# A head of dilated attention with its projections in another order, the joint softmax ahead of the gate, and scores split by batch

## The reference

```python
A_GROUPS = ((128, 1), (512, 4), (2048, 16))          # window, dilation; 8 heads of 128 each
proj = h @ w_in                                       # q, k, v of each group, and the gate
for g, (window, dil) in enumerate(A_GROUPS):
    o, lse = dilated_window_attention(q, k, v, slopes[g], window, dil)   # ALiBi bias, softmax in the window
wts = softmax(stack(lses), axis=0)                    # a joint softmax over the three groups
o = sum(wts[..., None] * stack(outs))
y = o * silu(gate)
return y @ w_out
```

## Time and profile before

| | |
|---|---|
| median of 3 runs | 1840.05 us (1839.97 to 1840.76) |
| the profiled execution's own time | 1839.34 us |
| its span, first to last instruction | 1837.6 us |
| TensorE matmuls busy | 1748.7 us, 95% |
| VectorE busy | 1085.2 us, 59% |
| ScalarE busy | 726.6 us, 40% |
| GpSimd busy | 400.3 us, 22% |
| mean granted TensorE clock | 0.98 of full |

### The profile page before, as it was taken

One profiled execution on the slowest core, in us unless ns is written; L12 is line 12 of the kernel. 1 busy time (PEld: TensorE's weight loads), 2 busy tenths in 40 slices (PEclk: granted clock), 3 DMA queues, 4 the chain that ended last, 5 costly groups with the idle time before them and its releaser, 6 DMA issues. The chain is left out here.

```text
span 1837.6 us, 24762 instructions
## 1 busy us (share of the span) xinstructions
PE 1748.7 (95%) x8848; PEld 1478.6 (80%) x8848; DVE 1085.2 (59%) x1878; ACT 726.6 (40%) x1465; POOL 400.3 (22%) x320
## 2 busy tenths in 40 slices
PE   6999999999999999999999999689898999999995
PEld 5888888888888888888888888578686788888884
DVE  5344365355355445455445534653797898988986
ACT  5223323313312322322322322342215877777774
POOL 1001001001001001000100100111003877777764
PEclk9999999999999999999999999889899999999997
DMA  4111111111111011111111110020100000000002
GB/s 160 47 35 69 35 35 69 35 35 58 34 46 57 34 34 57 34 37 66 34 34 57 35 58 0 1 99 1 46 24 26 27 26 26 26 26 26 6 7 109
DMA packets 23241, 76.75 MB, mean 42 GB/s; under 512 B 3088, under 2 KB 3216, under 8 KB 22928
## 3 DMA queue, kind: packets, MB, share of 16 engines
q1 hardware_dynamic: 23184, 75.98, 12.1%
HBM read 71.77 MB, written 4.19 MB: 41 GB/s over the span
## 5 line engine op out<-in xcount | busy, mean ns | idle before, releaser
L701 PE MATMUL bankA<-hTh,wh 128*128 128x512 f32 x1280 | 505.4, 395 | 0.4 <-DVE hTl L477 0.4
L701 PE MATMUL bankA<-hTh,wl 128*128 128x512 f32 x1280 | 499.2, 390 | 0.0
L701 PE MATMUL bankA<-hTl,wh 128*128 128x512 f32 x1280 | 498.4, 389 | 0.0
L701 PEld LDWEIGHTS bankA<-hTh,wl 128*128 128x128 f32 x1280 | 240.2, 188 | 51.6
L701 PEld LDWEIGHTS bankA<-hTh,wh 128*128 128x128 f32 x1280 | 240.4, 188 | 48.6 <-issue 1.1
L701 PEld LDWEIGHTS bankA<-hTl,wh 128*128 128x128 f32 x1280 | 240.6, 188 | 47.9
L293 POOL TENSOR_TENSOR prob<-prob,wt_blk 128x1024 f32<-128x1024 f32 x16 | 32.3, 2020 | 1074.9 <-DVE wt_blk L601 1074.9
L527 DVE TENSOR_TENSOR qkl<-bankA,qkh 128x512 fp32r<-128x512 f32 x96 | 66.4, 692 | 287.7 <-ACT qkh L355 287.4
L355 ACT ACTIVATE qkh<-bankA 128x512 fp32r<-128x512 f32 x96 | 57.3, 596 | 367.2 <-PE bankA L701 367.2
L613 DVE TENSOR_TENSOR X<-bankA,X 128x512 f32<-128x512 f32 x128 | 83.9, 685 | 52.8 <-PE bankA L794 52.8
L503 DVE TENSOR_TENSOR wl<-raw,wh 128x1024 fp32r<-128x1024 f32 x78 | 102.8, 1318 | 15.7 <-ACT wh L325 13.3
(11 more groups left out here) (208 smaller groups left out, 3594.5 us busy)
## 6 DMA issues: line engine op xcount, KB each, us to landing
raw<-a_w_in SPq DMA_DIRECT2D x80, 512.0 KB, 3.3
bias<-alibi SPq DMA_DIRECT2D x8, 512.0 KB, 3.3
raw_out<-a_w_out SPq DMA_DIRECT2D x8, 512.0 KB, 4.1
graw<-b_w_gate SPq DMA_DIRECT2D x8, 512.0 KB, 3.6
raw_o<-b_w_out SPq DMA_DIRECT2D x16, 256.0 KB, 2.6
raw_q<-b_w_q SPq DMA_DIRECT2D x8, 384.0 KB, 4.0
X<-x_prompt SPq DMA_DIRECT2D x4, 512.0 KB, 5.5
X<-x_sample SPq DMA_DIRECT2D x4, 512.0 KB, 8.8
```

The costliest lines, as they stand in the source:

```text
L701: ins = pe.matmul(proj_ps[b][:, :], w[a][:, slot, k * P:(k + 1) * P], hT[c][:, k, b * S:(b + 1) * S], start=(i == 0), stop=(i == last))
```

## The change

The blocks q2 and k2 move ahead of v1 and the gate. The joint softmax moves from the end of the head to the end of v1, so it stands in the queues ahead of the gate. s1 is scored for batch 0 after k1 and for batch 1 after the first batch of q2; s2 after k2 and after the first batch of v1; s0 after each batch of v0. A dilated tile takes two matmuls: the high query by the high and low keys side by side (256 columns), and the low query by the high keys added into the first half; VectorE adds the bias to the first half, then the second half. The output rows stand beside q2, k2, the gate and v2; w_out is split after k1. After the last head a list (`LAST_TURNS`) orders transposes, weighting, rows and squares, and the mean and power of the first batch are made there, not in the next stage.

```diff
-PROJ = ["q0", "k0", "v0", "q1", "k1", "v1", "gate", "q2", "k2", "v2"]
+PROJ = ["q0", "k0", "v0", "q1", "k1", "q2", "k2", "v1", "gate", "v2"]
-ROW_SLOTS = [("gate", 0), ("gate", 1), ("q2", 0), ("q2", 1), ("k2", 0), ("k2", 1), ("v2", 0), ("v2", 1)]
+ROW_SLOTS = [("q2", 0), ("q2", 1), ("k2", 0), ("k2", 1), ("gate", 0), ("gate", 1), ("v2", 0), ("v2", 1)]
-SUMS = {"s0": 0, "s1": 4, "s2": 6}
+SUMS = {"s0": 0, "s1": 4, "s2": 8}
+LAST_TURNS = [("v2", 0), ("v2", 1), ("turn", 0, 0), ("turn", 0, 1), ("weigh", 0, 0), ("turn", 0, 2), ("weigh", 0, 1),
+              ("turn", 0, 3), ("weigh", 0, 2), ("turn", 1, 0), ("weigh", 0, 3), ("gated", 0), ("turn", 1, 1),
+              ("weigh", 1, 0), ("turn", 1, 2), ("row", 0), ("row", 1), ("weigh", 1, 1), ("turn", 1, 3),
+              ("row", 2), ("row", 3), ("weigh", 1, 2), ("row", 4), ("row", 5), ("weigh", 1, 3), ("gated", 1),
+              ("square", 0), ("row", 6), ("row", 7), ("square", 1), ("square", 2), ("square", 3), ("rate", 0)]
+for i_last in range(NT // 2, NT):
+    LAST_TURNS += [("row", 2 * i_last), ("row", 2 * i_last + 1), ("square", i_last)]
...
-        qk = [sb(f"qk{s}", [P, 2, NB, S], F32R) for s in "hl"]
+        qk_parts = sb("qk", [P, 2, 2, NB, S], F32R)
+        qk = [qk_parts[:, part] for part in (HI, LO)]
...
-        row_ps = sum_ps + out_ps
+        row_ps = proj_ps + sum_ps
...
@@ GpSimd, after the last head
+            pool.wait_ge(mean_ready, NB + 1)
+            pool.tensor_tensor(after["rstd"][:, 0:QT], after["ms"][:, 0:QT], minus_half[:, 0:QT],
+                               ALU.pow).then_inc(rstd_ready, 1)
...
@@ ScalarE, head
-                        if name == "v2" and b == 0:
+                        if name == "v1" and b == 0:
                             exps(h, 1, [1])
...
-                    if name == "v1" and not is_first(h):
+                    if name == "k1" and not is_first(h):
                         split_out(h)
...
-                factors(h)
+                    if name == "v1":
+                        factors(h)
...
@@ VectorE
+            def take_dilated(h, kind, b, step):
+                g = int(kind[1])
+                src = bias[:, (5 + g) * P:(6 + g) * P].unsqueeze(1).broadcast_to((P, 2, P))
+                def halves(pair):
+                    ps = sum_ps[sum_slot(kind, 2 * b + pair)][:].rearrange("p (t z k) -> p t z k", t=2, z=2)
+                    return prob[:, 1, b, 2 * pair:2 * pair + 2, (g - 1) * P:g * P], ps
+                for pair in range(2):
+                    at = sum_no(h, kind, 2 * b + pair)
+                    dve.wait_ge(sum_done, at + 1)
+                    dst, ps = halves(pair)
+                    ins = dve.tensor_tensor(dst, ps[:, :, 0], src, ALU.add)
+                chain(ins, h, step)
+                for pair in range(2):
+                    dst, ps = halves(pair)
+                    dve.tensor_tensor(dst, ps[:, :, 1], dst, ALU.add).then_inc(sum_taken, 1)
+                return at
...
-                        if (name, b) in (("k2", 1), ("v2", 0)):
-                            at = take_scores(h, "s2", 1 - b)
-                            maxima(h, 1, slice(1 - b, 2 - b), at, 6 - b)
-                    if name == "v0":
-                        for n in range(4):
-                            at = take_scores(h, "s0", n)
-                    if name == "v1":
-                        for b in range(NB):
-                            take_scores(h, "s1", b)
+                        if (name, b) in (("k2", 1), ("v1", 0)):
+                            at = take_dilated(h, "s2", 1 - b, 5 - 2 * b)
+                            maxima(h, 1, slice(1 - b, 2 - b), at, 6 - 2 * b)
+                        if name == "v0":
+                            for n in (2 * b, 2 * b + 1):
+                                at = take_scores(h, "s0", n)
+                        if (name, b) in (("k1", 1), ("q2", 0)):
+                            take_dilated(h, "s1", 1 - b, 2 - b)
...
-                joint_softmax(h)
+                    if name == "v1":
+                        joint_softmax(h)
...
+                elif step[0] == "rate":
+                    dve.wait_ge(row_squared, QT)
+                    dve.tensor_scalar(after["ms"][:, 0:QT], after["ss"][:, 0:QT], 1.0 / D, RMS_EPS, ALU.mult,
+                                      ALU.add).then_inc(mean_ready, 1)
...
@@ TensorE, score and output
-                    b = n
+                    b, pair = n // 2, n % 2
                     pe.wait_ge(proj_taken[b], proj_no(h, "k" + kind[1]) + 1)
-                    for t in range(QT):
-                        cols = slice(t * P, (t + 1) * P)
-                        for m, (x, z) in enumerate(SPLIT_PRODUCT):
-                            ins = pe.matmul(ps[:, cols], qk[x][:, 0, b, cols], qk[z][:, 1, b, cols],
-                                            start=(m == 0), stop=(m == 2))
+                    for i in range(2):
+                        cols = slice((2 * pair + i) * P, (2 * pair + i + 1) * P)
+                        at = 2 * P * i
+                        pe.matmul(ps[:, at:at + 2 * P], qk[HI][:, 0, b, cols], qk_parts[:, :, 1, b, cols],
+                                  start=True, stop=True)
+                        ins = pe.matmul(ps[:, at:at + P], qk[LO][:, 0, b, cols], qk[HI][:, 1, b, cols],
+                                        start=False, stop=True, skip_group_check=True)
...
+                    if is_past(h):
+                        if i % QT == 0:
+                            pe.wait_ge(y_split, h * 2 - 1 + i // QT)
+                    elif r == 0:
                         pe.wait_ge(y_split, h * 2)
...
@@ stage_b_in, VectorE
-            rate(0)
-            dve.wait_ge(rstd_ready, 1)
             scale(0, 0)
             scale(0, 1)
```

More of the change, by code:

```diff
@@ L91, in rows_beside, with last_row @@
     return [(r, r // NT, r % NT) for r in (2 * at, 2 * at + 1)]
-def last_rows():
-    return [(2 * i + half, half, i) for i in range(NT) for half in range(2)]
+def last_row(r):
+    return r, r % 2, r // 2
+LAST_TURNS = [("v2", 0), ("v2", 1), ("turn", 0, 0), ("turn", 0, 1), ("weigh", 0, 0), ("turn", 0, 2), ("weigh", 0, 1),
[5 more added lines that the diff above has]
+    LAST_TURNS += [("row", 2 * i_last), ("row", 2 * i_last + 1), ("square", i_last)]
 def row_no(h, r):
@@ L443, in _, with last_square @@
             split_out(A_HEADS)
-            for name in ("q0", "k0", "v0", "q1"):
-                for b in range(NB):
-                    between(A_HEADS, name, b)
-            for i in range(NT):
+            def last_square(i):
                 act.wait_ge(row_taken, row_no(A_HEADS, 2 * i + 1) + 1)
+                if i == 0:
+                    act.wait_ge(turned, turn_no(A_HEADS, "p", 7) + 1)
                 if i >= QT:
@@ L452, in _ @@
                 act.activation(scaled_x[:, i % QT, :], X[:, i, :], ACT.Square,
-                               accum_out=next_ss[:, i:i + 1]).then_inc(row_squared, 1)
+                               accum_out=after["ss"][:, i:i + 1]).then_inc(row_squared, 1)
+            for step in LAST_TURNS:
+                if step[0] == "gated":
+                    take_gated(A_HEADS, step[1])
+                elif step[0] == "square":
+                    last_square(step[1])
+                else:
+                    stand_between(A_HEADS, step)
         @block.vector
@@ L531, in take @@
                     gb = gate[:, b, :]
[L532 to L533 removed]
+                    chain(dve.tensor_scalar(gb, gb, 1.0, None, ALU.add), h, 13 + 2 * b)
+                    chain(dve.reciprocal(gb, gb), h, 14 + 2 * b)
                     dve.tensor_tensor(gb, ps, gb, ALU.mult).then_inc(proj_taken[b], 1)
@@ L668, in _ @@
             split_out(A_HEADS)
[L669 to L672, removed]
+            for step in LAST_TURNS:
+                if step[0] == "gated":
+                    take_gated(A_HEADS, step[1])
+                elif step[0] == "row":
+                    add_rows(A_HEADS, [last_row(step[1])], row_ps)
+                elif step[0] == "rate":
+                    dve.wait_ge(row_squared, QT)
+                    dve.tensor_scalar(after["ms"][:, 0:QT], after["ss"][:, 0:QT], 1.0 / D, RMS_EPS, ALU.mult,
+                                      ALU.add).then_inc(mean_ready, 1)
+                else:
+                    stand_between(A_HEADS, step)
         @block.tensor
@@ L817, in head @@
                                 output(h, rows_beside(name, b), out_ps)
[L818 to L825, removed]
+                        if (name, b) in (("k2", 1), ("v1", 0)):
+                            for pair in range(2):
+                                score(h, "s2", 2 * (1 - b) + pair)
+                        if (name, b) in (("k1", 1), ("q2", 0)):
+                            for pair in range(2):
+                                score(h, "s1", 2 * (1 - b) + pair)
+                        if name == "v0":
+                            for n in (2 * b, 2 * b + 1):
```

(14 more changed lines are left out.)

89 lines of the change are left out of this document (46 added, 43 removed).

## The result

The changed kernel takes 1847.6 us, the median of six runs (1846.7 to 1849.17), beside 1840.74 for the kernel before on the same chip: a ratio of 1.0042, 95% interval 1.0031 to 1.0052. Forecast were 1847 and "slower". The profiled execution has a span of 1845.4 us at a mean granted clock of 0.977.

A forecast was written before the change was run, and what follows sets the result against it. TensorE, busy 95% of the span, was taken to bound the kernel. Gains of 29.7 against losses of 37.3 gave 7.6 lost on 1839.34, so 1846.9; forecast 1847 us, range 1838 to 1868.

The forecast's parts named there:

- The stall: Softmax ahead of the gate on VectorE: TensorE idles 3.1 at row 10 in seven heads, 3.9 in the first; 25.6 lost.
- T+13.4: When TensorE finishes gate batch 1 and asks for row 10; T is when ScalarE begins to empty v1's second batch.
- The clock: TensorE at half speed for 3.1 after half of the row waits: 6 us lost, bounds nothing and 12.
- Scores apart: Dilated tiles: one 256-column and one 128-column product replace three of 128; 12.6 us gained, bounds nothing and 14.1.
- Block scores: A whole projection between the two batches' pairs removes TensorE's wait for VectorE's emptying: 4.1 us gained.
- v1 without cover: v1's transposes directly follow v1's projection, so the second batch's wait for ScalarE's copy: 0.44 x 8 = 3.5 us lost.
- Two more returns: Two more returns per head to a projection after transposes, 5.58 instead of 5.44: at most 2.2 us lost.
- End of the stage: Last projection to next stage's first scaling: earlier probability transposes and reordered row adds; 13 us gained, bounds 9.8 and 16.
- Rival 2: GpSimd's weighting holds VectorE up at the gate: 15 more idle and 6 more for the clock, 1868; chance 0.17.
- Rival 3: VectorE reaches row 8 before TensorE asks for row 10, so no wait arises: 24 gained, 1816; chance 0.12.

The follow-up runs named there:

- the filled wait: The changed kernel with 12 matmuls of 512 columns (16 in the first head), results unused, ahead of waiting row 10: 1834.52 us, ratio 0.9975.
- the kernel with the softmax under v2: The changed kernel with the joint softmax and ScalarE's `factors` moved behind the row adds of v2's first batch: 1811.44 us, ratio 0.9846.

## Why the prediction was right

The forecast, the stall with some of its clock, came true, and for the reason given: one place in VectorE's queue made the stall. That the time came within 1 us of 1847 is luck: the clock took twice what was forecast, and errors the other way cancelled it.

- *The stall*: forecast 7 x 3.1 + 3.9 = 25.6, measured 21.0 + 3.9 = 24.9. The row adds came when the working said; TensorE asked 0.27 later (568.91, where T+13.4 is 568.64).
- *The clock*: the term that was mis-sized, 6 forecast, 11 to 12 by the filled wait, the upper bound. Six stalls of eight lost the clock, not half of them, and the first two for longer (windows at 0.72 and 0.74, the other four at 0.87 or 0.88). The half came from a row that was read too short: of the idle that began at 1386.6 the prediction says that the clock held through it until 1390.4. But that idle lasted until 1393.92, and at 1390.4 the clock fell within it:

```profile
1393.92 0.80 PE L1670 MATMUL bankC<-cqTh,wqh 128*128 128x512 f32 x1 [7.39 <-DVE wql L1560]
```

So the row shows no idle that the clock outlasted. Nor would 3.8 at full clock have settled a stall of 3: four of the six falls came after TensorE had resumed.

- *Scores apart*: forecast 12.6; (1.31 - 0.87) x 32 batches is 14.1, the upper bound, and cutting the product again lost about 13 (1860.76 - 1847.6). The "1.8 to 1.9" that the prediction gives for eight products is its sum for sixteen, both batches.
- *Block scores*: the wait of 4.1 is gone, as forecast. *v1 without cover*: from the first transpose to the next projection 1.33 instead of 0.81 (555.04 to 556.37), 4.2 in eight heads, where 3.5 was forecast; the waits in it sum to 2.4. *Two more returns* do not show as the 2.2 allowed for: without the stall, a head of the kernel with the softmax under v2 lasts 141.33 (984.62 to 1125.95, ScalarE's copies of v2), before 143.50: 2.2 shorter, where these terms gave 1.4. Added up over a head from start to start of TensorE's matmuls, the dilated scores take 1.8 less and the block scores 0.8 less (3.8 before, 3.0 now; only their wait, 0.5, had been counted), the transposes 0.45 more, and projections and rows 0.1 less. That is all of the 2.2, and no return is in it.
- *A stall costs more than its wait*: a head in which the clock held lasts 144.7, 3.4 more than 141.33, for a wait of 2.98. The list counts from the last matmul's end (568.91), where the next one would have begun 0.227 after its start, at 568.75; and the first step after the wait is 0.33.
- Together: at the last copy of v2 the changed kernel is 1170.95 - 1148.23 = 22.7 behind; the working gives 20.6. With the softmax under v2 this copy is at 1132.75, so the terms other than stall and clock gained 15.5 where 11.0 was forecast, and stall and clock lost 38.2 where 31.6 was forecast. The two errors, 4.5 and 6.6, mostly cancel each other.
- *End of the stage*: 13.0 forecast and measured, partly by another way than the working's. The old order alone gives 50.33 - 35.88 = 14.45: the idle 11.96 - 2.29 = 9.7, as forecast; then 1.9 from the second gated product to the first row add (2.00 instead of 3.88, where TensorE idled and came back at half clock), 1.9 in the sixteen adds (9.9 instead of 11.8) and 1.1 to the scaling. The new order did not give its 3: with the early rate it cost 1.4 in these executions.
- 22.7 - 13.0 = 9.7 at the start of the next stage; the span ends 7.8 later. The 1.9 that the next stage gives back were not forecast. In its first 25 us the granted clock is 0.73 before (1198.56 to 1223.56) and 0.86 after (1208.26 to 1233.26), which fits; no run tests it.

Rival 2 fell as priced (reciprocals 3.353 to 3.355 in all sixteen; the gate's add 0.43 to 0.51 but for one of 1.70 in the first head, before which GpSimd had started), though its mechanism exists where GpSimd starts first. Rival 3's 1816 is, within 5, what the change is worth with the stall removed by hand: 1811.

## What to carry to other kernels

When work moves ahead in one engine's queue, lay out the queue behind it with its lengths and compare it with the moment at which the busiest engine asks: start times from the trace before gave the new stall to 0.3 us. A stall on a TensorE that is otherwise dense costs more than its length; here half as much again (38.2 for waits of 24.9). A row that is to show that the clock holds has to be followed past the end of the idle. A step put early because its result is wanted early holds up all that stands behind it if its input is late: the rate, waiting 2.3 with eight adds behind it, cost 1.9, and the reordering around it gained nothing that shows.

## What was not expected of the hardware

Four of the six falls of the clock came after TensorE had already resumed, 0.4 to 1.4 later: at 571.89 it went on at full clock (1.00 from 572.00 to 572.25, 0.59 in the quarter after that, then 0.50), and the clock was half until about 575.7. And equal stalls behaved unequally: after 2.98 and 2.98 idle (restarts at 427.18 and 1010.83) the clock held at 1.00, after 2.98 to 3.01 at 571.89, 718.18, 864.49 and 1155.44 it fell.
